# Hybrid decoder step: SSD gating on GpSimd, scaled sample states behind the first SSD addition, four U blocks kept on chip, spread loads

## The reference, cut to what matters

```
proj = rmsnorm(x) @ w_in ; z, xbc, dt, gate, xl = split(proj)
xs, bm, cm = silu(conv(xbc))
y, ssd_state = ssd_chunked(xs, dt, a, bm, cm, h0)      # 4 chunks of 128 tokens
y_ssd = rmsnorm((y + d_skip * xs) * silu(z))
y_lru = rmsnorm(lru_scan(...) * gelu(gate))
h = h + concat(y_ssd, y_lru) @ w_out
h = h + peer(rmsnorm(h))        # 16384 experts, 8 heads, top 16
h = h + rmsnorm((p @ w_ple_proj) * sigmoid(rmsnorm(h) @ w_ple_gate))
y = rmsnorm(h)
```

## Time and profile before

| what | value |
|---|---|
| three runs | 1800.72, 1799.42, 1797.62 us; median 1799.42 |
| the profiled execution: its time, and its span | 1798.23 us, 1796.5 us |
| busy: PE, PEld, DVE, ACT, POOL | 97%, 95%, 84%, 47%, 30% |
| PE busy, mixer's end, 265 to 306 us | 30.61 of 41 us |
| PE busy, U blocks, 520 to 1020 us | 496.21 of 500 us |
| PE busy, 1020 to 1120 us | 100.00 of 100 us |
| DMA share and rate, 520 to 1020 us | 0.77, 277 GB/s |
| DMA share and rate, 1020 to 1120 us | 0.96, 356 GB/s |
| DMA share and rate, 1480 to 1600 us | 1.04, 396 GB/s |
| ring load Rw<-vn, median from issue to landing | 13.2 us |
| PE's wait at tile 45 for DVE's first ssd_add (h, L1092) | 4.4 us, once |
| sample_decay on DVE at step 37, two instructions from 277.75 us | 0.8 us |

### The profile page before, as it was taken

The page is one execution under the profiler, slowest core; times in us unless marked ns, Lnnn a source line. Parts: engine busy times, 40 slices in busy tenths (PEclk is TensorE's granted clock), DMA queues, the critical chain, the costliest instruction groups (busy, mean ns, idle before and its releaser), DMA issues.

```text
span 1796.5 us, 29704 instructions
## 1 busy us (share of the span) xinstructions
PE 1733.9 (97%) x11346; PEld 1700.0 (95%) x11346; DVE 1512.7 (84%) x2750; ACT 836.7 (47%) x1206; POOL 543.6 (30%) x416
## 2 busy tenths in 40 slices
PE   7999997899999999999999999899999989999996
PEld 6999996789999999999999999899999989999995
DVE  6757999867768779999999999779888979899777
ACT  5556652434333333357777777423233233333163
POOL 3100220000000012344444444344554535555300
PEclk9999999999999999999999999999999999999998
DMA  4212342134345556789999999999999999999611
GB/s 157 94 64 79 135 147 95 65 129 170 121 137 158 179 177 232 254 304 354 370 362 376 347 359 368 400 393 396 396 396 397 396 393 396 396 397 391 212 59 51
DMA packets 164254, 462.70 MB, mean 258 GB/s; under 512 B 17201, under 2 KB 77169, under 8 KB 161425
## 3 DMA queue, kind: packets, MB, share of 16 engines
q1 hardware_dynamic: 118032, 293.00, 44.9%
q0 software_dynamic: 46080, 167.79, 24.8%
HBM read 405.39 MB, written 55.34 MB: 256 GB/s over the span
## 4 chain that ended last, share of the span: by engine, by line
PE 68%; DVE 15%; DMA 12%; ACT 2%; issue 2%; POOL 0%; SPq 0%; DVEq 0%; ACTq 0%
PE PS L470 12%; PE PS L1608 7%; PE PS L1621 7%; PE PS L1623 7%; PE PS L1622 7%; PE PS L1609 7%; PE PS L1610 7%; DMA Rw<-vn 6%; PE PS L1591 5%; PE PS L1679 3%; DMA ug<-un,idxU 3%; DVE Rl L170 2%; DVE ug L2020 2%; PE PS L2227 2%; DMA ug<-vn,idxU 1%
## 5 line engine op out<-in xcount | busy, mean ns | idle before, releaser
L165 ACT CAST Rh<-Rw 128x1024 fp32r<-128x1024 f32 x272 | 284.4, 1046 | 351.7 <-DMA Rw<-vn 294.5
L170 DVE TENSOR_TENSOR Rl<-Rw,Rh 128x1024 fp32r<-128x1024 f32 x272 | 331.9, 1221 | 100.0 <-ACT Rh L165 99.1
L1567 POOL DMA_INDIRECT ug<-un,idxU x160 | 241.2, 1508 | 526.2 <-DVE dots L2020 345.1
L1621 PE MATMUL PS<-Hh,Rh 128*128 128x384 f32 x1024 | 344.3, 336 | 7.7 <-DVE Rl L170 6.0
L1608 PE MATMUL PS<-Xh,Rh 128*128 128x384 f32 x992 | 343.4, 346 | 8.5 <-ACT Ab L1719 5.5
L1622 PE MATMUL PS<-Hl,Rh 128*128 128x384 f32 x1024 | 343.0, 335 | 0.0
L1623 PE MATMUL PS<-Hh,Rl 128*128 128x384 f32 x1024 | 342.9, 335 | 0.0
L1609 PE MATMUL PS<-Xl,Rh 128*128 128x384 f32 x992 | 334.8, 338 | 0.0
L1610 PE MATMUL PS<-Xh,Rl 128*128 128x384 f32 x992 | 334.0, 337 | 0.0
L1567 POOL DMA_INDIRECT ug<-vn,idxU x160 | 256.0, 1600 | 224.6 <-DVE yacc L2025 165.6
L1621 PEld LDWEIGHTS PS<-Hh,Rh 128*128 128x128 f32 x1024 | 193.0, 188 | 9.9 <-DVE Rl L170 6.3
(11 more groups left out here) (440 smaller groups left out, 3112.8 us busy)
## 6 DMA issues: line engine op xcount, KB each, us to landing
Rw<-uw SPq DMA_DIRECT2D x144, 512.0 KB, 4.6
Rw<-vn SPq DMA_DIRECT2D x128, 512.0 KB, 13.2
Wr<-wm SPq DMA_DIRECT2D x51, 512.0 KB, 3.3
acts<-Ab SPq DMA_DIRECT2D x128, 192.0 KB, 5.4
gates<-stg SPq DMA_DIRECT2D x12, 2048.0 KB, 9.8
Aq<-acts SPq DMA_DIRECT2D x32, 768.0 KB, 16.6
Gq<-gates SPq DMA_DIRECT2D x31, 768.0 KB, 16.2
L<-acsd SPq DMA_DIRECT2D x4, 1024.0 KB, 6.9
```

The costliest lines, as they stand in the source:

```text
L165: a.copy(self.Rh[:, q, :], self.Rw[:, q, :]).then_inc(self.S("rhi"), 1)
L170: v.tensor_tensor(self.Rl[:, q, :], self.Rw[:, q, :], self.Rh[:, q, :].bitcast(F32), ALU.subtract).then_inc(self.S("rlo"), 1)
L1567: p.indirect_dma_start(out=ug[:, r % 4, :], out_offset=None, in_=un if r < IDC else vn, in_offset=bass.IndirectOffsetOnAxis(ap=idxU[:, r % ...
L1621: pe.matmul(out, Rh[:, q, w], hh, start=(g == 0), stop=False)
```

## The change

- **y_gate moves to GpSimd.** Its eight multiplications of 128x512 stand at the end of POOL's program of the mixer, in the order of the chunks. ACT, which reads their result in step 41, now waits for the last chunk's halves one by one.
- **sample_decay moves** from DVE's step 37 to step 35.
- **The states' scaling moves** on DVE from step 43 to step 44, behind recip(2) and ssd_add(0); sample_add(0) and (1) follow it.
- **spread_e(3) moves** on SP from step 41 to step 40, behind an added wait for DVE's carry(2).
- **The last four U blocks** (g = 124 to 127) are neither stored nor loaded: ACT writes their gelu to Aq[2], and VGRP makes their group the third that the V blocks use. The V weights are loaded in that order. The gates of the second pair of groups are no longer neighbours and come in four DMAs of 384 KB, in pieces of 128 numbers.
- **At the turn** SP's first gate loads move one step earlier (136, 137), h_hi(0) of ACT from 140 to 141, h_full(0) of DVE from 140 to 141, h_lo(0) from 141 to 142.
- **The three early loads** are issued in front of ring loads 215, 219 and 223 instead of together in front of 214.

```diff
+KEEP = 1
+VGRP = [0, 1] + list(range(PK // 4 - KEEP, PK // 4)) + list(range(2, PK // 4 - KEEP))
@@ Ring.load
+            b = 4 * VGRP[(m - NIT) // 4] + m % 4
+            src = self.vn[b * P:(b + 1) * P, :]
@@ mixer, sync
+            if n == 40:
+                sp.wait_ge(S("ymm"), 2)
+                sp.wait_ge(S("cem"), 3)
+                spread_e(3)
             if n == 41:
-                sp.wait_ge(S("ymm"), 2)
-                spread_e(3)
@@ mixer, pool
+        for c in range(NC):
+            for b in range(2):
+                g.wait_ge(S("yad"), 2 * c + b + 1)
+                g.tensor_tensor(xs[:, 4 * b:4 * b + 4, chunk(c)], xs[:, 4 * b:4 * b + 4, chunk(c)],
+                                sz[:, 4 * b:4 * b + 4, chunk(c)], ALU.mult).then_inc(S("yg"), 1)
@@ mixer, scalar
             if n == 41:
                 a.wait_ge(S("ymm"), NC)
-                a.wait_ge(S("yg"), 2 * NC)
                 for k in range(ND):
+                    a.wait_ge(S("yg"), 2 * (NC - 1) + k // 4 + 1)
@@ mixer, vector
             if n == 37:
                 l_min(2)
-                y_gate(0)
-                sample_decay()
...
             if n == 35:
...
+                sample_decay()
...
             if n == 43:
...
-                v.tensor_tensor(s0s[:, :, :, :], s0s[:, :, :, :],
...
-            if n == OS0 + 1:
-                sample_add(0)
-                sample_add(1)
...
                 ssd_add(n - OS0 - 1)
+                if n == OS0 + 1:
...
+                    v.tensor_tensor(s0s[:, :, :, :], s0s[:, :, :, :],
...
+                    sample_add(0)
+                    sample_add(1)
@@ experts
+    LOADS = [NIT + 71, NIT + 75, NIT + 79]
@@ experts, sync
-            if n >= 0 and u_of(n) is not None:
+            if n >= 0 and u_of(n) is not None and u_of(n) < PK - 4 * KEEP:
                 store_act(u_of(n))
-            if m == NIT + 70:
-                early[0](sp)
+            if m in LOADS:
+                early[0](sp, LOADS.index(m))
-            if n == GEND - 2:
+            if n == GEND - 3:
...
                 load_g(0, 0)
-            if n == GEND - 1:
+            if n == GEND - 2:
                 load_g(0, 1, NGB - 1)
-            if n == GEND + 2:
-                load_a(2)
@@ experts, scalar
+            if g >= PK - 4 * KEEP:
+                a.wait_ge(S("gmm"), NU)
+                a.wait_ge(S("gw0"), 16 * (NGB // 2))
+                a.activation(Aq[VGRP.index(g // 4)][:, g % 4, :], PS[:, g % 2, 0:DT], ACT.Gelu_apprx_tanh
+                             ).then_inc(S("glu"), 1)
+                return
-            if n == GEND + 1:
+            if n == GEND + 2:
                 h_hi(0)
@@ experts, vector
             if n == GEND + 1:
                 last_gates()
+            if n == GEND + 2:
                 h_full(0)
-            if n == GEND + 2:
+            if n == GEND + 3:
                 h_lo(0)
```

More of the change, by code:

```diff
@@ L156, in load @@
             sp.wait_ge(self.S("rlo"), m - 3)
-        src = self.uw[m, :, :, :].rearrange("p k j -> p (k j)") if m < NIT else self.vn[(m - NIT) * P:(m - NIT + 1) * P, :]
+        if m < NIT:
+            src = self.uw[m, :, :, :].rearrange("p k j -> p (k j)")
+        else:
+            b = 4 * VGRP[(m - NIT) // 4] + m % 4
+            src = self.vn[b * P:(b + 1) * P, :]
         sp.dma_start(self.Rw[:, q, :], src).then_inc(self.S("rw%d" % q), 16)
@@ L1065, in y_sum @@
                 m.then_inc(S("yad"), 1)
[L1067 to L1071, removed]
         def lru_add(d):
@@ L1176, in vector @@
                 y_sum(3)
-                y_gate(3)
             if OL0 <= p < OS0:
@@ L1185, in vector @@
                 l_min(2)
-                y_gate(0)
-                sample_decay()
             if n == 38:
                 l_min(3)
-                y_gate(1)
-            if n == 39:
-                y_gate(2)
             if n == 1:
@@ L1373, in vector @@
                 ssd_add(n - OS0 - 1)
+                if n == OS0 + 1:
+                    v.wait_ge(S("ymm"), NC + 1)
+                    v.wait_ge(S("abs"), 64)
+                    v.tensor_tensor(s0s[:, :, :, :], s0s[:, :, :, :],
+                                    ces[:, :, LB - 1:32:LB].unsqueeze(3).broadcast_to([P, HG, NB, HD]), ALU.mult
+                                    ).then_inc(S("s0d"), 1)
+                    v.wait_ge(S("s0d"), 1)
+                    sample_add(0)
+                    sample_add(1)
                 if n >= OS0 + 3:
@@ L1496, in load_a @@
                 sp.wait_ge(S("wmm"), max(VI, VI + 4 * i - 16))
+            b = VGRP[i]
             for s in range(4):
-                sp.wait_ge(S("as%d" % s), 16 * (i + 1))
-            sp.dma_start(Aq[i % 5][:, :, :], acts[4 * i:4 * i + 4, :, :].rearrange("i p t -> p i t")
+                sp.wait_ge(S("as%d" % s), 16 * (b + 1))
+            sp.dma_start(Aq[i % 5][:, :, :], acts[4 * b:4 * b + 4, :, :].rearrange("i p t -> p i t")
                          ).then_inc(S("aq%d" % (i % 5)), 16)
@@ L1504, in load_g @@
             r = slice(0, NGB // 2) if part == 0 else slice(NGB // 2, nb)
-            sp.dma_start(Gq[o % 2][:, r, :], gates[r, :, 8 * o:8 * o + 8, :].rearrange("b p i t -> p b (i t)")
+            if o == 1:
+                for s in range(2):
+                    b = 4 * VGRP[2 + s]
+                    sp.dma_start(Gq[1][:, r, 4 * GTK * s:4 * GTK * s + 4 * GTK],
+                                 gates[r, :, b:b + 4, :].rearrange("b p i t -> p b (i t)")).then_inc(S("gq1"), 16)
+                return
+            b = 4 * VGRP[2 * o]
+            sp.dma_start(Gq[o % 2][:, r, :], gates[r, :, b:b + 8, :].rearrange("b p i t -> p b (i t)")
                          ).then_inc(S("gq%d" % (o % 2)), 16)
@@ L2002, in h_full @@
         def h_full(i):
-            v.wait_ge(S("aq%d" % (i % 5)), 16 * (i // 5 + 1))
-            v.wait_ge(S("gq%d" % ((i // 2) % 2)), 32 * (i // 4 + 1))
+            if 2 <= i < 2 + KEEP:
+                v.wait_ge(S("glu"), 4 * VGRP[i] + 4)
+            else:
+                v.wait_ge(S("aq%d" % (i % 5)), 16 * (i // 5 + (0 if 2 <= i % 5 < 2 + KEEP else 1)))
+            v.wait_ge(S("gq%d" % ((i // 2) % 2)), 32 * (i // 4 + 1) + 32 * ((i // 2) % 2))
             v.tensor_tensor(Aq[i % 5][:, :, :].rearrange("p i (b t) -> p i b t", b=NGB),
@@ L2144, in gate_bank, with early_sync @@
         return PS[:, BANK[i % 6], 0:HT]
-    def early_sync(sp):
-        sp.wait_ge(S("wmm"), NIT)
-        sp.wait_ge(S("sdt"), IDC)
-        sp.wait_ge(S("gmm"), NU)
-        sp.dma_start(praw[:, :, :], pT).then_inc(S("ple_in"), 16)
-        sp.dma_start(wpr[:, :, :], w_plp).then_inc(S("ple_in"), 16)
-        sp.dma_start(Wr[0][:, :, :], w_plg[0, :, :, :]).then_inc(S("ple_in"), 16)
+    def early_sync(sp, part):
+        if part == 0:
+            sp.wait_ge(S("wmm"), NIT)
+            sp.wait_ge(S("sdt"), IDC)
+            sp.wait_ge(S("gmm"), NU)
+            sp.dma_start(praw[:, :, :], pT).then_inc(S("ple_in"), 16)
+        elif part == 1:
+            sp.dma_start(wpr[:, :, :], w_plp).then_inc(S("ple_in"), 16)
+        else:
+            sp.dma_start(Wr[0][:, :, :], w_plg[0, :, :, :]).then_inc(S("ple_in"), 16)
     def early_scalar(a, part):
```

5 lines of the change are left out of this document (removed).

## The result

| | before | changed |
|---|---|---|
| median of five runs each, us | 1799.42 (1796.64 to 1800.72) | 1788.25 (1785.89 to 1792.88) |
| ratio, with its 95% interval | | 0.9943 (0.9931 to 0.9955) |
| profiled execution: time, span | 1798.23, 1796.5 | 1788.25, 1786.5 |

The change makes the kernel faster. By the medians it gives 11.2 us, by the ratio 10.3 us (8.1 to 12.4), where the prediction's median of 1784.3 meant 15.1 (range 1776 to 1791). The sign and the range held; about 4 to 5 us of the expected gain did not come. The spans differ by 10.0 us, where the prediction's sum said 14.3.

The account below looks back on a forecast made before the run. PE, busy 97%, could gain only from gaps, with V blocks bound by DMA. Mixer 6.9, bytes 3.0 and spread 5.4 less 1.0 gave 14.3 us, the turn's 5.3 absorbed: 1783.9, stated as 1784.3 us, range 1776 to 1791.

Parts of the forecast that it names:

- The mixer, 6.9 us: Mixer's end: 0.9 us from moving gating and decay off DVE plus 6.0 us from moving the states' scaling.
- 0.9 for gating and ce: Scan, chunk 3: scores start earlier without y_gate(1) and the wait for ce, until exps(3) on ACT limits them; 0.9 us.
- 6.0 for the scaling: Tile 45: its wait of 4.4 us goes and the clock stays up, 1.6 us; between 4.5 and 6.0.
- room of 4.1 us beside POOL: Scan, 268.5 to 272.57: DVE reads only PSUM beside SBUF, so POOL's two gating halves, 2.6 us, cost nothing.
- R3: Rival, chance 0.04: POOL's multiplications lock out DVE; slower above 4.5 us a half, 1805 us at 5.5.
- The turn, 5.3 us on PE: From U to V blocks: gates land earlier, first V block near 1155 instead of 1160.41; 3.0 us if gates land late.
- h_lo(0) ends near 1155: At the turn: DVE finishes the first product's low part then, so the first V block starts 5.3 us earlier.
- Bytes, 3.0 us: V blocks' DMA: 1.57 MB fewer bytes save 4.0 us, less 1.0 us for gates in small pieces.
- pieces: Gate loads: 1.57 MB in pieces of 512 B instead of 1 KB cost 1.0 us, bounds nothing and 4.0.
- The spread, 5.4 - 1.0 = 4.4 us: V blocks: splitting the early loads gains DMA's 5.4 us lead at block 262, less PE's 1.0 us behind DMA.
- R1: Rival, chance 0.12: PE sets the pace in V, DMA can exceed 396 GB/s, all 21.4 us come: 1777 us.
- R2: Rival, chance 0.12: V blocks give nothing; three waits with halved clock eat turn and bytes, only 6.9 us remain: 1791.

Follow-up runs that it names:

- b_keep: Kernel before with only the four kept U blocks, gate loads in pieces and the turn one item later, early loads together; 1796.54 us, ratio 0.9982.
- a_hlo: Changed kernel with h_lo(0) right behind h_full(0) on DVE instead of one item later; 1786.60 us, ratio 0.9937.
- b_gate: Kernel before with only y_gate on POOL, sample_decay at step 35 and spread_e(3) at step 40; 1797.38 us, ratio 0.9991.
- b_scale: Kernel before with only the states' scaling and sample_add(0), (1) behind recip(2) and ssd_add(0); 1793.68 us, ratio 0.9969.
- a_late: Changed kernel with the three early loads in front of ring loads 255, 259 and 263, their splits at items 268 to 270; 1784.51 us, ratio 0.9923.
- a_all: Changed kernel with h_lo(0) behind h_full(0), early loads in front of 255, 261 and 265, and gathered rows until item 270; 1786.20 us, ratio 0.9940.

## Why the prediction was right or wrong

- **The mixer, 6.9 us: right.** 0.9 for gating and ce measured 1.6 (0 to 3.2), 6.0 for the scaling 5.6 (3.4 to 7.7). POOL's half took some 1.27 us for the 1.3 taken, the exponentials were what was late next, and tile 46 had the 0.1 us to spare. One reading in it was wrong and cost nothing: the room of 4.1 us beside POOL was read at chunk 1, and behind chunk 3 h<-h,tmpL follows y_sum sooner. There POOL held DVE for 0.8 us. So R3's mechanism is real, and R3 was out by its price: it needed 4.5 us a half.
- **The turn, 5.3 us on PE: wrong, and without harm.** V block 0 came 6.9 us earlier, 4.6 of these from above, so 2.3 from the turn, and half the clock behind the wait left 0.4 at V block 1. The step that failed is "h_lo(0) ends near 1155": in b_keep, whose mixer is not shifted, it ended at 1160.3. The sum did not price the two rows of u that stand in front of it on DVE, each behind its gather. a_hlo puts it right, and shows why it does not matter: the sum had it that DMA takes this gain back, and so it was: of the 6.1 us that a_hlo gains at V block 1 beyond its U blocks, nothing is left at block 213, and 1 us end to end by the ratios, U blocks included.
- **Bytes, 3.0 us: right as far as shown.** b_keep, which holds the turn too, gives 3.2 (1.6 to 4.9), pieces 0.8 us a pair where 1.0 was taken.
- **The spread, 5.4 - 1.0 = 4.4 us: wrong, and this is the gap.** It measured -0.5 us alone and nothing inside the changed kernel. The step was "the rest gave DMA a lead over PE that it never needed", read at block 262. By there the lead grows by itself: it was 2.4 us at block 255 in the same trace (not the 4 us to spare that R1's text gives to block 222 and later), 0.2 in b_gate, b_scale, b_keep and the changed kernel, and there it is again 4.6 at block 262, where the sum had 1.0 ("PE follows DMA at some 1.0 us"). The sum had DMA nearly right there: the low part of block 262 came at 1648.2 for its 1646.8. It had PE wrong: 1652.9 for its 1647.8. So the lead at 262 is not what the early loads cost PE, and the sum should have been made at the last block that DMA holds up. Without this term it gives 14.3 - 4.4 = 9.9 us, and 10.3 were measured.
- **The figures given for the median.** The sum gives 1783.9, and with the 1.2 us that the text adds for the median 1785.1, not 1784.3. In the same way R1's 21.4 us would be 1778.0, not 1777, and R2's 6.9 us 1792.5, not 1791. That the forecast's band (1778 to 1789) holds 1788.25 is in part luck: the sum of the terms that were borne out, 9.9 us, gives 1789.5, just outside it.
- **R1, PE sets the pace: half true.** In the changed kernel PE runs from block 145 to 213 without a wait (4.16 us a block), but a_hlo, where PE comes earlier, waits there. Behind the early loads it is DMA. R1 would have needed both stretches.
- **R2, waits with half the clock:** they did not come; the longest behind V block 0 was 1.7 us, and the clock stayed at 1.00 from 1400 to 1480 us.

## What to carry to other kernels

Where a transfer stream and an engine are balanced, ask at which item the engine last waits for the stream, and add up the bytes due by then. Here only taking bytes away before that item helped, and moving them about did not, unless they could go behind it (a_late). Then ask the same of the end: work that was put off there must be in before the last item, and a gain of 11 us at block 255 can shrink to 7 within sixteen blocks (a_all). Read a lead or a margin in more than one execution before it becomes a term.
